# Third product's addition, block 4's suffix sums and the shift of the output projection's half 0 in a one-core encoder step

## What is computed

```python
tail = lax.cumsum(log_keep, axis=3, reverse=True) - log_keep            # stick-breaking attention
weight = jnp.where(visible, jnp.exp(jax.nn.log_sigmoid(z) + tail), 0.0)
...
mix = jax.nn.sigmoid(ga) * (pool_out @ w_br_pool) + jax.nn.sigmoid(gb) * (attn @ w_br_attn)
h = _layer_norm(ALPHA * h + (mix @ w_out + b_out), ln1_g, ln1_b)
f = jnp.square(jax.nn.relu(h @ w_mlp1 + b_mlp1)) @ w_mlp2 + b_mlp2
h = _layer_norm(ALPHA * h + f, ln2_g, ln2_b)
```

## Time and profile before

| | us |
|---|---|
| median of 3 runs (815.38 to 815.93) | 815.79 |
| the profiled execution | 818.31 |
| its span | 816.4 |
| TensorE matmuls busy | 800.0 |
| TensorE weight loads busy (beside matmuls) | 768.5 |
| VectorE busy | 499.8 |
| ScalarE busy | 389.0 |
| GpSimd busy | 100.3 |

### The profile page before, as it was taken

One profiled execution on the slowest core, in us unless ns is written; L12 is line 12 of the kernel. 1 busy time (PEld: TensorE's weight loads), 2 busy tenths in 40 slices (PEclk: granted clock), 3 DMA queues, 4 the chain that ended last, 5 costly groups with the idle time before them and its releaser, 6 DMA issues.

```text
span 816.4 us, 14503 instructions
## 1 busy us (share of the span) xinstructions
PE 800.0 (98%) x5879; PEld 768.5 (94%) x5879; DVE 499.8 (61%) x843; ACT 389.0 (48%) x646; POOL 100.3 (12%) x120
## 2 busy tenths in 40 slices
PE   7999999999999999999999999999999999999994
PEld 5899889999989899999999999999999999999994
DVE  4833344654435466874968678774767877445644
ACT  4632445555545465563645654333554433344324
POOL 2100000470000000007540000000000000000354
PEclk9999999999999999999999999999999999999998
DMA  7732231112121111233111214222221422222203
GB/s 272 258 143 79 77 112 52 52 56 65 46 72 52 53 52 52 86 122 130 52 53 53 74 56 155 79 104 78 79 71 58 155 78 104 79 77 78 78 1 116
DMA packets 23081, 71.61 MB, mean 88 GB/s; under 512 B 2464, under 2 KB 6704, under 8 KB 22640
## 3 DMA queue, kind: packets, MB, share of 16 engines
q1 hardware_dynamic: 22336, 68.23, 25.2%
q0 software_dynamic: 544, 2.52, 0.9%
q10 hardware_dynamic: 144, 0.07, 0.1%
HBM read 65.96 MB, written 4.85 MB: 87 GB/s over the span
## 4 chain that ended last, share of the span: by engine, by line
PE 96%; DVE 2%; ACT 1%; DMA 1%; issue 0%; SPq 0%; ACTq 0%; DVEq 0%
PE lin L604 14%; PE lin L605 14%; PE lin L606 14%; PE z L1068 6%; PE z L1070 5%; PE z L1071 5%; PE z L841 3%; PE lin L973 3%; PE lin L974 3%; PE lin L975 3%; PE lin L1089 2%; PE lin L1088 2%; PE lin L1087 2%; PE z L827 1%; PE z L902 1%; PE lin L724 1%
## 5 line engine op out<-in xcount | busy, mean ns | idle before, releaser
L604 PE MATMUL lin<-h_hi,whi 128*128 128x288 f32 (+1 forms) x832 | 247.2, 297 | 0.0
L605 PE MATMUL lin<-h_lo,whi 128*128 128x288 f32 (+1 forms) x832 | 245.9, 296 | 0.0
L606 PE MATMUL lin<-h_hi,wlo 128*128 128x288 f32 (+1 forms) x832 | 245.0, 294 | 0.0
L606 PEld LDWEIGHTS lin<-h_hi,wlo 128*128 128x128 f32 x832 | 156.6, 188 | 0.0
L604 PEld LDWEIGHTS lin<-h_hi,whi 128*128 128x128 f32 x832 | 156.4, 188 | 0.1
L605 PEld LDWEIGHTS lin<-h_lo,whi 128*128 128x128 f32 x832 | 156.4, 188 | 0.1
L1772 DVE TENSOR_TENSOR wlo<-raw,whi 128x1024 fp32r<-128x1024 f32 x65 | 81.0, 1246 | 34.8 <-ACT whi L1162 30.0
L1162 ACT ACTIVATE whi<-raw 128x1024 fp32r<-128x1024 f32 x58 | 60.9, 1051 | 50.4 <-PE lin L606 32.5
L1565 ACT ACTIVATE relu_t<-lin,vecs 128x288 f32<-128x288 f32 x60 | 30.1, 501 | 91.4 <-PE lin L606 88.0
L2196 DVE TENSOR_TENSOR relu_sq<-relu_t 128x288 f32<-128x288 f32 x60 | 27.5, 458 | 64.7 <-ACT relu_t L1565 64.7
L1068 PE MATMUL z<-f_ops,whi 128*128 128x288 f32 x216 | 64.0, 296 | 1.0 <-issue 1.0
(11 more groups left out here) (339 smaller groups left out, 1893.2 us busy)
## 6 DMA issues: line engine op xcount, KB each, us to landing
raw<-w_stream SPq DMA_DIRECT2D x88, 512.0 KB, 3.4
w_set<-w_sets SPq DMA_DIRECT2D x32, 384.0 KB, 3.8
r<-x_t SPq DMA_DIRECT2D x8, 296.0 KB, 6.0
kcache<-k_cache SPq DMA_DIRECT2D x1, 2048.0 KB, 9.8
vcache<-v_cache SPq DMA_DIRECT2D x1, 2048.0 KB, 10.3
y<-r SPq DMA_DIRECT2D x8, 160.0 KB, 1.8
k_new<-k_t POOLq DMA_DIRECT2D x1, 1184.0 KB, 4.8
v_new<-v_t POOLq DMA_DIRECT2D x1, 1024.0 KB, 5.2
```

The source lines that it names most:

```text
L604: pe.matmul(out, w_h, hi, start=first, stop=False)
L605: pe.matmul(out, w_h, lo, start=False, stop=False)
L606: return pe.matmul(out, w_l, hi, start=False, stop=last)
```

## The change

Three edits. In `suffix_sums` the fp32 matmuls of block 4 with `tri` are gone, and the fp32r ones of block 3 with `tri_r` take block 4's 16 columns along. In `out_pass` the shifting matmul of units 1 to 7 is left out in half 0, and VectorE adds the shift to the residual chunks instead, each before the unit itself is added (`shifted1`). In both MLP passes VectorE's addition of product 2 comes before the low part of operand 4 and no longer behind it.

```diff
--- before.py
+++ after.py
@@ -302,8 +302,8 @@
         n0_mean, n0_guess, n0_rstd = sem("n0_mean"), sem("n0_guess"), sem("n0_rstd")
         n0_centred_v, n0_centred_g, n0_scaled, n0_hi, n0_lo = (
             sem("n0_centred_v"), sem("n0_centred_g"), sem("n0_scaled"), sem("n0_hi"), sem("n0_lo"))
-        n1_prep1, n1_prep, n1_first, n1_shift, n1_d0 = (
-            sem("n1_prep1"), sem("n1_prep"), sem("n1_first"), sem("n1_shift"), sem("n1_d0"))
+        n1_prep1, n1_prep, n1_first, n1_shift, n1_d0, n1_shifted = (
+            sem("n1_prep1"), sem("n1_prep"), sem("n1_first"), sem("n1_shift"), sem("n1_d0"), sem("n1_shifted"))
         n1_sq, n1_sum, n1_sumsq, n1_terms = sem("n1_sq"), sem("n1_sum"), sem("n1_sumsq"), sem("n1_terms")
         n1_msq, n1_mean, n1_var, n1_guess, n1_rstd = (
             sem("n1_msq"), sem("n1_mean"), sem("n1_var"), sem("n1_guess"), sem("n1_rstd"))
@@ -854,18 +854,16 @@
                 late, w = is_late(i), LATE_W if is_late(i) else EARLY_W
                 for p in range(2):
                     pe.wait_ge(splo_done, pieces_before(i) + p + 1)
-                    for b in ((4, 3), (2,))[p] if late else ((1,), (0,))[p]:
+                    for b in ((3,), (2,))[p] if late else ((1,), (0,))[p]:
                         for e in range(2):
                             dst = z_of(e, b)
-                            if b < 4:
-                                last = subtract(dst, tri_r, sp_of(e, b), QW[b])
+
+                            last = subtract(dst, tri_r, sp_of(e, b), QW[3] + QW[4] if b == 3 else QW[b])
                             if b < 3:
                                 last = subtract(dst + QS[b + 1] - QS[b], below_r, sp_of(e, b + 1), QW[b + 1])
-                            if b >= 3:
-
-                                const = tri if b == 4 else below
-                                at, src = dst + QS[4] - QS[b], e * w + LATE_AT[4]
-                                last = pe.matmul(zf[:, at:at + QW[4]], const[:, :], sa[:, src:src + QW[4]],
+                            else:
+                                at, src = dst + QS[4] - QS[3], e * w + LATE_AT[4]
+                                last = pe.matmul(zf[:, at:at + QW[4]], below[:, :], sa[:, src:src + QW[4]],
                                                  start=False, stop=True, skip_group_check=True)
                     last.then_inc(tri_done, 1)
 
@@ -993,14 +991,16 @@
                         if m == 0:
                             pe.wait_ge(mix_lo_done, 2 * k + h + 1)
                         last = kept(bank, out_home(m), k, mix_hi[:, k, c], mix_lo[:, k, c], k == 0,
-                                    m == 0 and k == KC - 1)
-                    if m:
+                                    (m == 0 or h == 0) and k == KC - 1)
+                    if m and h:
                         if m == 1:
-                            pe.wait_ge(ones_made, 1)
                             pe.wait_ge(n1_first, h + 1)
                         last = pe.matmul(bank, ones_r[:, :], first_r[:, c], start=False, stop=True)
                     last.then_inc(unit_done if h else half_done, 1)
                     if m == 1:
+                        if h == 0:
+                            pe.wait_ge(ones_made, 1)
+                            pe.wait_ge(n1_first, 1)
                         pe.matmul(r1_shift(h), ones_r[:, :], first_r[:, c], start=True, stop=True)\
                             .then_inc(n1_shift, 1)
                     if h == 1 and m == 0:
@@ -2139,9 +2139,17 @@
                 if h == 0:
                     dve.wait_ge(half_done, N_OUT + m + 1)
                     dve.wait_ge(n1_prep, m + 1)
+                    if m:
+                        dve.wait_ge(n1_shifted, m)
                 else:
                     dve.wait_ge(unit_done, U_OUT + m + 1)
                 tt(r1[:, m, half(h)], lin[:, m % 2, 0:HA], r1[:, m, half(h)], ALU.add).then_inc(bank_free[m % 2], 1)
+
+            def shifted1(m):
+
+                dve.wait_ge(n1_shift, 1)
+                dve.wait_ge(n1_prep, m + 1)
+                tt(r1[:, m, half(0)], r1_shift(0), r1[:, m, half(0)], ALU.add).then_inc(n1_shifted, 1)
 
             def first_shifted(h):
 
@@ -2236,11 +2244,16 @@
 
             split_out(2)
             for m in range(KC):
+                if m == 1:
+                    shifted1(1)
                 out_half(m, 0)
                 if m in (1, 2):
                     residual_lo(5 + m)
                 if m == 1:
                     first_shifted(0)
+                    shifted1(2)
+                if m and m + 2 < KC:
+                    shifted1(m + 2)
                 if m + 3 < KC:
                     split_out(m + 3)
             out_half(0, 1)
@@ -2376,8 +2389,11 @@
                     sum_lo(s, o, PRS - 1)
                 for o in range(3, OPS * GROUPS):
                     g, q = divmod(o, OPS)
-                    if o > 3:
+                    if o > 3 and o != 5:
                         add_op(s, o - 3)
+                    if o == 4:
+
+                        add_op(s, 2)
                     op_lo(s, o)
                     if g and q == 0:
                         weight_sum(s, g, 2)
```

## The result

| | before | after |
|---|---|---|
| median of the comparison (us) | 815.59 (814.65 to 815.99, 6 runs) | 811.51 (810.7 to 813.25, 6 runs) |
| the profiled execution | 818.31 | 810.72 |
| its span | 816.4 | 808.8 |
| granted clock over the span | 0.993 | 0.996 |

The ratio is 0.9948, interval [0.9935, 0.9961]: 4.2 us less, between 2.9 and 5.3. Forecast were 2.80 less and 813.0. The measured median is at the low end of the range, which the prediction writes as 811.5; its own terms (815.79 - 1.44 - 1.84 - 0.92) give 811.59. So the direction was right and the size too small.

The account below looks back on a forecast made before the run. TensorE, busy 98% of the span, was taken as the bound. Savings of 0.98 + 1.64 + 0.18 = 2.80 us off the 815.79 median gave 813.0, range 811.5 to 814.6.

Parts of the forecast that it names:

- Part A: Both MLP passes, product 2's addition moved forward: 0.72 us stall removed, 0.23 lost at product 5; 0.49 a pass, 0.98 in sum.
- so pass two counts the same: Step in Part A: the wait list shows two equal waits, one per pass, so pass two also gains 0.49 us.
- ends 0 and 1.44: Range of Part A's gain: 0 us if the wait only moves, 1.44 at most.
- Rival 2: MLP passes: Part A's wait only moves, to product 5; 0.98 us less gain, 814.0; chance 0.12.
- rival 3: Part B's first saving given back in item 4, Part C at its lower end, Part A at half: 814.5; chance 0.11.
- rival 4: Output projection, half 0: VectorE becomes the bound, each shift stretched and in TensorE's way; slower, 819.6; chance 0.04.
- rival 5: Suffix sums: TensorE's pace is set by something other than the tri matmuls; 1.16 us remain, 814.6; chance 0.04.
- Part B: Suffix sums of four late items: two fp32 tri matmuls fewer each, 0.41 us an item, 1.64 in sum, ends 1.44 and 1.84.
- Part C: Output projection, half 0: seven matmuls fewer, 0.92 us, mostly lost to stalls before units 4 and 5; gain 0.18.
- The second stall of 0.26: Output projection, half 0: TensorE waits 0.26 us before unit 5, whose bank VectorE frees late after unit 4's shift and a split.
- Rival 1: Output projection, half 0: Part C's 0.92 us won in full, 0.74 more than forecast, 812.25; chance 0.22.
- part C's lower end: Output projection, half 0: -0.4 us, if GpSimd's adds stretch both VectorE splits by another 0.3.

Follow-up runs that it names:

- run 2: Kernel before with only VectorE's addition of product 2 moved ahead of operand 4's low part, in both passes; 813.33 us, ratio 0.998.
- Run 5: The changed kernel, unaltered, compared a second time with the kernel before; 812.47 us against 815.84, ratio 0.9957.
- Run 9: Changed kernel, but in half 0 VectorE shifts units 4 to 7 only and units 1 to 3 keep their matmul; 812.43 us against 814.88, ratio 0.9962.
- run 7: Changed kernel with chunk 0's shift first in half 0, other shifts one unit later, residual low parts behind splits; 812.55 us, ratio 0.9958 to kernel before.
- run 12: Run 9's kernel with product 3's addition also ahead of operand 5's low part, timed a second time; 811.4 us against 815.25, ratio 0.9957.

## Why the prediction was wrong, and where it was right

**Part A: the step that failed is "so pass two counts the same".** It put 0.49 on pass two because the stall there is as long as pass one's in the list of waits. The distance between products, which I took from pass one (2.36), is 2.38 to 2.40 in pass two of the kernel before from the stall on. Those rows were in the trace of before, and the sum had no term for them. In run 2 and in the change's first profile pass two ran at 2.360 and gave 1.11 instead of 0.49: 0.6 us more than forecast. Run 5 shows that this is not simply what the edit is worth. The same code had the slow rhythm in both passes there, part A gave 0.4 instead of 0.98, and the whole 2.25. So the prediction had one pace for two passes where each can have either, and in the changed kernel's two profiles the edits give 3.45 and 2.25 by the trace. What was in reach was the range: part A's "ends 0 and 1.44" should have had an upper end of 2.0 or so.

**Part A's stall: right.** Forecast 0.49 a pass, by the trace 0.48 and 0.49 at the products concerned. The new wait is at product 5, as long as forecast (0.15), and product 6 did not wait. Rival 2 (the wait only moves) fell, and so did rivals 3, 4 and 5.

**Part B: right.** 0.41 an item forecast, 0.44 measured, so the weight loads' 0.46 was the nearer row. The 16 columns cost nothing, though the 0.15 between two starts, from which the prediction read this, is not the loads' pace: those loads are 0.11 apart in the kernel before (162.04 and 162.15 us), and 0.11 or 0.13 in the change. Item 4 gave back 0.18 against a forecast of nothing with ends of -0.4 and +0.5. 1.64 forecast, 1.59 by the trace.

**Part C: right in kind, and near in size by luck.** The chain through unit 1's two new additions, chunk 0's shift and ScalarE made TensorE wait before unit 4, as forecast. Its slip was sized 0.48 and measured 0.60, so unit 4 came 0.59 late and not 0.43. The second stall of 0.26 did not come. It had counted on unit 5's split being stretched to 1.83 as before; GpSimd adds at other times when the splits move, and this one took 1.47. The two errors nearly cancel: 0.18 forecast, 0.26 by the trace. Rival 1 fell: the seven matmuls' 0.92 were not won. Run 9 shows the reason from the other side, since four of them without a shift in the way were won in full.

**What contention did.** The shifts and the units' additions, with one PSUM and one SBUF input, took 0.44 to 0.46 with and without GpSimd's additions beside them. Splits and residual low parts have two SBUF inputs. In the change's half 0 a split took 1.23 alone, or when it began ahead of the GpSimd addition beside it (the one at 364.35; GpSimd's then took 1.50, where others take 0.80), and 1.47 to 1.87 when it began behind one; a residual low part took 0.75 alone and 0.98 behind one (1.35 in run 7). The Trainium skill (SBUF — State Buffer, Who interferes with whom) says that a VectorE instruction with at most one SBUF input doesn't contend with GpSimd and that one with two does, with an instruction of GpSimd that reads SBUF. The trace agrees. Neither says beforehand which of the splits will be hit. The prediction added that the sum would then lie nearer to part C's lower end; it did not.

**The rest of the 4.2 is open.** The edits make 2.83 by the terms that I had (1.59 + 0.26 + 0.98), and the forecast was 2.80. With the better rhythm in pass two they make 3.45. The first comparison says 4.2 [2.9, 5.3], the second 3.5 [2.4, 4.6], and both hold 3.45; the forecast's 2.80 is just outside the first and inside the second. What lies beyond 3.45 in the first may be the start: five of its six runs of the changed kernel had a granted clock of 0.996 or more, and runs of the unchanged kernel with such a clock take 814.6 in the median (26 runs) against 815.8 for the rest (36 runs). That is argued from the grouping, and no run forced a start; nor is it known how many executions had which rhythm. The range's lower end was every part's best case with nothing for either.

**Open.** What begins the slow rhythm. It went with the stall in pass two five times out of five, never held in pass one of the old order, and came in both passes of runs 5 and 9 and in pass two of run 12 with new orders. Loads lead their matmuls by 0.130 in it and by 0.128 otherwise, which says that the spacing differs and not why.

## What to carry to other kernels

Before you price a stall in the second of two equal stages, compare the pace of the work behind it in both: a list of waits shows no rhythm. Before you compare two single profiles, align the starts of the same instructions and look at the difference where the diff has not yet acted; here more than half of it was there. Take a stall's size from the distance between starts: the idle time that the profile names was 0.16 less than the delay here. And work moved off a full engine is won only from the point where the engine that takes it has slack: four shifts placed behind that point gave twice what seven did.

## What the runs showed of the hardware

- A stream of matmuls in which the profile shows no wait runs at one of two paces for the rest of a stage: 288 columns each 0.131 us (2.360 for 18) or 0.133 (2.379 to 2.401 for 18), at the same granted clock. The slower one came in 10 of the 23 passes in which VectorE had held back a weight load, by as little as 0.015 us, and in none of the five without.
- In the kernel before's profile the addition for one input chunk started 1.6 us later, TensorE idled 1.65 us, and the granted clock was 0.50 (1.2 GHz) from 9 to 12 us; with a second such stretch the start was 3.9 us longer.
- Two fp32r matmuls of 144 or 160 columns start 0.07 to 0.16 us apart, while their weight loads are 0.11 to 0.13 apart.
- After a wait the next 18 matmuls take about 0.08 more than their 2.36 (2.436 and 2.444), and the next 24 of the output projection 3.24 instead of 3.16.
- A weight load that waits for an addition of VectorE starts 0.07 us after the addition's end, in every such wait of the Winograd passes.
